# Modulation products moved from the rounds of the attentions to the merges of branches, half a group behind the gates of a half branch

## What is computed

```python
# first block, once
gates = jax.nn.sigmoid(proj("gates").reshape(b, s, N_BRANCH, D_MODEL) + b_gate[l])
projected = jnp.einsum('bsnc,ncd->bsnd', branches, w_branch[l])
mixed = jnp.sum(gates * projected, axis=2)
# second block, per layer i (DEPTH_2 = 2)
mod = jax.nn.silu(c) @ w_ada[i] + b_ada[i]
sh1, sc1, gt1, sh2, sc2, gt2 = jnp.split(mod[:, None, :], N_MOD, axis=-1)
modc = jax.nn.silu(c_ctx) @ w_ada[i] + b_ada[i]
ga, gb, gc = jnp.split(jax.nn.sigmoid(gates), N_BRANCH_2, axis=-1)
m = ga * (ya @ w_branch[0]) + gb * (yb @ w_branch[1]) + gc * (yc @ w_branch[2])
```

## Time and profile before

| | |
|---|---|
| median of 3 executions | 3238.53 us (3232.24 to 3244.42) |
| the profiled execution's own time | 3241.71 us |
| its span, first to last instruction | 3239.9 us |
| mean granted TensorE clock | 0.925 |
| busy: PE, PE weight loads, DVE, ACT, POOL | 82%, 55%, 36%, 27%, 1% of the span |
| DMA | 669.19 MB, mean 207 GB/s |
| modulation matmuls (L1499) | 192, in the trace as 384 records, 49.6 us busy |

### The profile page before, as it was taken

How to read it: one execution, slowest core, us unless ns; L and a number is a source line. 1 busy time by engine, 2 the same in 40 slices (tenths; PEclk the granted TensorE clock), 3 DMA queues, 4 the chain that set the end, 5 groups by cost and what they waited for, 6 DMA issues and landing times. The chain is left out here.

```text
span 3239.9 us, 36546 instructions
## 1 busy us (share of the span) xinstructions
PE 2658.2 (82%) x14364; PEld 1796.3 (55%) x14364; DVE 1169.5 (36%) x1596; ACT 882.3 (27%) x1314; POOL 39.9 (1%) x36
## 2 busy tenths in 40 slices
PE   6887898998998787889977778887887896787876
PEld 5666687998996464668753222223664894222222
DVE  4446544655753334344432001103444552000001
ACT  3344433544442232322221000002233432000001
POOL 0100000000000000000000000000000001000000
PEclk8888998999998898889978999998897997999999
DMA  4463532453542333112215999996211343999996
GB/s 154 157 257 113 198 130 92 178 185 123 188 159 91 150 136 130 50 69 100 85 46 224 404 405 407 403 414 260 78 52 50 142 165 147 413 410 409 411 410 269
DMA packets 92935, 669.19 MB, mean 207 GB/s; under 512 B 10320, under 2 KB 10496, under 8 KB 12800
## 3 DMA queue, kind: packets, MB, share of 16 engines
q1 hardware_dynamic: 90256, 654.67, 51.6%
q0 software_dynamic: 2272, 11.52, 1.0%
q10 hardware_dynamic: 272, 1.05, 0.1%
HBM read 666.13 MB, written 1.06 MB: 206 GB/s over the span
## 5 line engine op out<-in xcount | busy, mean ns | idle before, releaser
L1860 PE MATMUL ps<-ring,WK 128*64 128x512 f32 x3072 | 731.0, 605 | 171.2 <-DMA ring<-in_stream 147.1
L424 PE MATMUL ps<-A,piece_hi 128*128 128x256 f32 (+1 forms) x1952 | 618.5, 317 | 97.7 <-DVEq L358 33.1
L376 DVE TENSOR_TENSOR ring_lo<-ring,piece_hi 128x1024 fp32r<-128x1024 f32 x378 | 459.3, 1220 | 450.4 <-ACT piece_hi L369 449.3
L425 PE MATMUL ps<-A,piece_hi 128*128 128x256 f32 (+1 forms) x1952 | 612.5, 314 | 0.0
L426 PE MATMUL ps<-A,ring_lo 128*128 128x256 f32 (+1 forms) x1952 | 611.7, 313 | 0.0
L1860 PEld LDWEIGHTS ps<-ring,WK 128*64 128x64 f32 x3072 | 194.5, 137 | 674.2 <-DMA ring<-in_stream 371.9
L424 PEld LDWEIGHTS ps<-A,piece_hi 128*128 128x128 f32 x1952 | 384.7, 197 | 129.3 <-issue 59.2
L369 ACT ACTIVATE piece_hi<-ring 128x1024 fp32r<-128x1024 f32 x378 | 388.2, 1053 | 223.8 <-DVEq L450 131.9
L425 PEld LDWEIGHTS ps<-A,piece_hi 128*128 128x128 f32 x1952 | 385.6, 198 | 17.2
L426 PEld LDWEIGHTS ps<-A,ring_lo 128*128 128x128 f32 x1952 | 384.9, 197 | 18.1
L1980 DVE TENSOR_TENSOR WK<-WK,ps 128x512 f32<-128x512 f32 x32 | 22.0, 688 | 636.7 <-PE ps L1860 636.7
(11 more groups left out here) (252 smaller groups left out, 2447.6 us busy)
## 6 DMA issues: line engine op xcount, KB each, us to landing
ring<-in_stream SPq DMA_DIRECT2D x621, 1024.0 KB, 7.7
WK<-in_na_bias POOLq DMA_DIRECT2D x2, 2048.0 KB, 7.8
WK<-cum_scratch POOLq DMA_DIRECT2D x1, 2048.0 KB, 9.7
const<-in_const SPq DMA_DIRECT2D x1, 1267.0 KB, 11.7
WK<-in_x SPq DMA_DIRECT2D x1, 1024.0 KB, 5.4
WK<-in_mem SPq DMA_DIRECT2D x1, 1024.0 KB, 9.1
WK<-cum_scratch POOLq DMA_DIRECT2D x1, 1024.0 KB, 14.9
WK<-in_lru_w POOLq DMA_DIRECT2D x1, 1024.0 KB, 5.1
```

Of the source, the lines that this page charges most:

```text
L376: nc.vector.tensor_tensor(ring_lo[:, slot, at:at + PIECE], ring[:, slot, at:at + PIECE], f32(piece_hi[:, j, :]), ALU.subtract).then_inc(lo ...
L424: nc.tensor.matmul(out_, l[0], r[0], start=first, stop=False)
L425: nc.tensor.matmul(out_, l[0], r[1], start=False, stop=False)
L1860: last = nc.tensor.matmul(ps[64 * n:64 * n + 64, bank, :], lhs, piece[:, n * 512:n * 512 + 512], start=(k == 0), stop=(k == DC - 1))
```

## The change

The modulation products leave the attentions. They are done in the merges, in halves of a group: 8 raw pieces (k = 0 to 3 or 4 to 7) between the four gate banks and the four branch banks of a half branch. The first layer's groups go into half branches 1 to 6 of the first block's merge, the second layer's groups into half branches 0 to 5 of the merge in the second block's first layer. A group's turn (four matmuls, L1487) comes one half branch later, behind that half's raw pieces. The stream has its pieces in the new order. During these two merges the other banks go round a ring of six, since 6 and 7 belong to the modulation. The first block's merge is written out in place of its loop.

```diff
+ADA_HALF = 8
+ADA_MERGE = {0: (1, 2, 3, 4, 5, 6), 1: (0, 1, 2, 3, 4, 5)}
...
     for n in range(4):
         for h in range(2):
             fm(w_in, g0 + n * D + h * 512, g0 + n * D + h * 512 + 512)
+            ada(0, 2 * n + h)
             fm(x["w_branch"][0, n], h * 512, h * 512 + 512)
...
+        def merge_pe(pe, cur, branches, kc, n, ada=None):
             yh, yl = y_split(kc, n)
+            for i in range(branches):
                 for h in range(2):
+                    at = 2 * i + h
                     fm_banks(pe, cur, in_a()(n), n, 4)
+                    if ada is not None and ada_half(ada, at) is not None:
+                        ada_half_pe(pe, cur, ada, ada_half(ada, at))
+                    if ada is not None and ada_full_before(ada, at) is not None:
+                        ada_turn_pe(pe, 3 * ada + ada_full_before(ada, at) // 2)
                     if h == 0:
                         pe.wait_ge(y_lo, cur.base("y") + 1 + i)
                     fm_banks(pe, cur, lambda k: (yh[:, k, :], yl[:, k, :]), n, 4, kc)
-            merge_loop(pe, cur, branches, kc, one_branch)
+            if ada is not None and ada_full_before(ada, 2 * branches) is not None:
+                ada_turn_pe(pe, 3 * ada + 2)
...
 (merge_act)
                         read_bank(act, cur, True, op, piece=True)
+                    if ada is not None and ada_half(ada, 2 * i + h) is not None:
+                        past_raw(act, cur, ADA_HALF)
                     skip_fm(act, cur, 4, kc)
...
 (merge_dve)
                 for h in range(2):
+                    full = None if ada is None else ada_full_before(ada, 2 * i + h)
                     skip_fm(dve, cur, 4)
+                    if ada is not None and ada_half(ada, 2 * i + h) is not None:
+                        past_raw(dve, cur, ADA_HALF)
+                        if ada_half(ada, 2 * i + h) % 2 == 1:
+                            ada_rows_dve(dve, cur, ada, ada_half(ada, 2 * i + h))
...
+        def ada_half_pe(pe, cur, layer, half):
+            assert cur.p == ADA_PIECE[layer, half]
+            n, b = 3 * layer + half // 2, 6 + (3 * layer + half // 2) % 2
+            if half % 2 == 0:
                 pe.wait_ge(cs_ready, 1)
+                if n >= 2:
+                    pe.wait_ge(ada_added, n - 1)
+            for k in range(4 * (half % 2), 4 * (half % 2) + 4):
+                for q in range(4):
+                    if q % 2 == 0:
+                        piece = raw_piece(pe, cur)
+                        behind = cur.p - 1 - ADA_PIECE[layer, half]
+                        if behind < 4:
+                            pe.wait_ge(bank_free[cur.bank(cur.g - 4 + behind)], cur.bank_use(1, cur.g - 4 + behind))
+                    last = nc.tensor.matmul(ps[32 * q:32 * q + 32, b, :], CS[:, k, :], piece[:, q % 2 * 512:q % 2 * 512 + 512],
+                                            start=(k == 0), stop=(k == DC - 1))
+                    if (k, q) == (DC - 1, 3):
+                        last.then_inc(ada_full, 1)
+                    elif q % 2 == 1:
+                        raw_used(last, cur)
...
+        def ada_rows_dve(dve, cur, layer, half):
+            n = 3 * layer + half // 2
             dve.wait_ge(ada_full, n + 1)
+            dve.sem_inc(piece_used[(ADA_PIECE[layer, half] + ADA_HALF - 1) % 4], 1)
             if n > 0:
                 dve.wait_ge(ada_turned, n)
+            nc.vector.tensor_copy(ROWS[:, :], ps[:, 6 + n % 2, :]).then_inc(ada_taken, 1)
...
-            fox_pe(pe, cur, ada_with_pe(pe, cur, "fox"))
+            fox_pe(pe, cur)
...
-            merge_pe(pe, cur, 4, DC, T)
+            cur.set_ring(range(6))
+            merge_pe(pe, cur, 4, DC, T, ada=0)
+            cur.set_ring(range(NB))
```

More of the change, by code:

```diff
@@ L136, in __init__ @@
         self.g = 0
+        self.places = []
+        self.ring = list(range(NB))
+        self.turn = 0
+        self.uses = [0] * NB
         self.i = None
@@ L157, in split_use, with place, set_ring, used @@
         return v if self.i is None else v + self.i * (self.pieces_per // 4)
-    def bank(self):
-        return self.g % NB
-    def bank_use(self, k=0):
-        v = self.g // NB + k
+    def place(self, g):
+        while len(self.places) <= g:
+            b = self.ring[self.turn % len(self.ring)]
+            self.places.append((b, self.uses[b]))
+            self.uses[b] += 1
+            self.turn += 1
+        return self.places[g]
+    def set_ring(self, banks):
+        while len(self.places) < self.g:
+            self.place(len(self.places))
+        assert len(self.places) == self.g, (self.who, len(self.places), self.g)
+        self.ring, self.turn = list(banks), 0
+    def used(self, bank):
+        self.place(self.g - 1)
+        return sum(b == bank for b, _ in self.places[:self.g])
+    def bank(self, g=None):
+        return self.place(self.g if g is None else g)[0]
+    def bank_use(self, k=0, g=None):
+        v = self.place(self.g if g is None else g)[1] + k
         return v if self.i is None else v + self.i * self.banks_per
+    def taken_before(self):
+        return self.place(self.g)[1] > 0
 def one(i):
@@ L485, in tm_tile @@
         def tm_tile(pe, cur, t0, tt):
-            banks = [(cur.g + m) % NB for m in range(tt)]
+            banks = [cur.bank(cur.g + m) for m in range(tt)]
             for j in range(4):
@@ L1286, in lru_dve @@
             steps(nc.vector.tensor_tensor(LY, LXC[:, :, :], LG[:, :, :], ALU.mult))
-        def merge_loop(eng, cur, branches, kc, one_branch, steps=None, per=0):
-            if 2 * (4 + kc // 2) % (2 * R) == 0:
-                with loop(eng, cur, branches, pieces=2 * (4 + kc // 2), banks=16, steps=steps, steps_per=per) as i:
-                    one_branch(i)
-            else:
-                for i in range(branches):
-                    one_branch(i)
         def y_split(kc, n):
@@ L1351, in one_branch @@
                     dve.drain().then_inc(gate_used, 1)
-            merge_loop(dve, cur, branches, kc, one_branch, steps=steps, per=8)
+                    if full is not None:
+                        ada_add_dve(dve, 3 * ada + full // 2)
+            if ada is not None and ada_full_before(ada, 2 * branches) is not None:
+                ada_add_dve(dve, 3 * ada + 2)
             cur.add("merge", 2 * branches)
@@ L1508, in ada_rows_dve, with ada_turn_pe @@
+        def ada_turn_pe(pe, n):
+            pe.wait_ge(ada_taken, n + 1)
+            pick = ident.rearrange("p (q r) -> p q r", q=4)[:, :, 0:2]
+            for c in range(4):
+                last = nc.tensor.matmul(ps[:, 6 + n % 2, 8 * c:8 * c + 8], ROWS[:, c * P:(c + 1) * P], pick, start=True, stop=True)
+            last.then_inc(ada_turned, 1)
+        def ada_rows_dve(dve, cur, layer, half):
+            n = 3 * layer + half // 2
             dve.wait_ge(ada_full, n + 1)
-            dve.sem_inc(piece_used[(ADA_PIECE[layer, g] + ADA_GROUP - 1) % 4], 1)
+            dve.sem_inc(piece_used[(ADA_PIECE[layer, half] + ADA_HALF - 1) % 4], 1)
@@ L1561, in gmod_dve, with ada_full_before @@
+        def ada_full_before(layer, at):
+            half = ada_half(layer, at - 1)
+            return half if half is not None and half % 2 == 1 else None
         def gmod_dve(dve, steps, g, which):
@@ L2108, in _ @@
                 barrier(pe, cur)
-                att_pe(pe, cur, da_x, **({"after": ada_with_pe(pe, cur, "da_x")} if layer == 0 else {}))
+                att_pe(pe, cur, da_x)
                 barrier(pe, cur)
@@ L2193, in _ @@
                 barrier(act, cur)
-                att_act(act, cur, steps, na_x, **({"after": ada_with_act(act, cur, "na_x")} if layer == 0 else {}))
+                att_act(act, cur, steps, na_x)
                 barrier(act, cur)
                 if n > T:
-                    att_act(act, cur, steps, na_ctx, ada_with_act(act, cur, "na_ctx"))
+                    att_act(act, cur, steps, na_ctx)
                     barrier(act, cur)
@@ L2200, in _ @@
                 barrier(act, cur)
-                att_act(act, cur, steps, da_x, **({"after": ada_with_act(act, cur, "da_x")} if layer == 0 else {}))
+                att_act(act, cur, steps, da_x)
                 barrier(act, cur)
@@ L2287, in _ @@
                 dve.wait_ge(loads, 16 * LOADS["nab"][layer])
[L2288 removed]
+                att_dve(dve, cur, steps, na_x)
                 barrier(dve, cur)
                 if n > T:
[L2291 removed]
+                    att_dve(dve, cur, steps, na_ctx)
                     barrier(dve, cur)
@@ L2296, in _ @@
                 barrier(dve, cur)
-                att_dve(dve, cur, steps, da_x, **({"after": ada_with_dve(dve, cur, "da_x")} if layer == 0 else {}))
+                att_dve(dve, cur, steps, da_x)
                 barrier(dve, cur)
```

235 lines of the change are left out of this document (87 added, 148 removed).

## The result

| | before | changed |
|---|---|---|
| median of the runs that were compared | 3235.39 us (3227.95 to 3244.42, 4 runs) | 3311.02 us (3307.26 to 3322.69, 4 runs) |
| the profiled execution's own time | 3241.71 us | 3307.26 us |
| its span | 3239.9 us | 3305.1 us |
| mean granted TensorE clock | 0.925 | 0.919 |
| DMA | 669.19 MB | 669.34 MB |

The changed kernel is slower by 75.6 us, a ratio of 1.0239 with a 95% interval of 1.02 to 1.0278. The two profiled executions lie 65.2 us apart in span, since the one of before is slow for its kernel (3241.71 against a median of 3235.39) and the one of after fast for its own (3307.26 against 3311.02).

The account below looks back on a forecast made before the run. TensorE was taken as busiest everywhere, hardly resting in the merges, waiting on DVE and ACT in the attentions. Merges losing 147.8 us less 51.5 gained gave +96 on 3241.7: 3338, by the median 3335 us; range 3288 to 3370 (0.85).

Parts of the forecast that it names:

- The stall in the merges: Each of twelve half branches starts its branch 10.3 us after its gates, not 3.64; 123.6 us lost.
- R3: Last raw slot of a half branch, loaded only once the gates end; lands at T + 5.3, PE idle 2.5 us.
- B0: First branch slot, queued behind R3; lands at T + 7.8, is then split, and the branch starts at T + 10.3.
- 14 us or less from the last gate matmul to full rate: Sign expected in each of the twelve half branches of the merges.
- The clock: Rests before merge branches slow their matmuls: 2.4 us per narrow branch, 1.8 per wide; 25.2 us lost, lower bound 0.
- The rival by which the clock holds: Raw work between the two merge rests keeps the clock up, so 25.2 us fall away: 3310 us, chance 0.25.
- Turns and the unrolled loop: Merges: two group turns on the path cost 2.1 us; unrolling the first merge gives back 3.1 us.
- The attentions: All 192 modulation products leave fox, sb, na_x, na_ctx and da_x; 51.5 us gained after 4.4 for splits.
- I take 4.7: Time of a bare fox round, between 3.6 and 5.9 us; fox gains 21.1 us, bounds 12.7 and 28.8.
- na_ctx, 4.5 taken: Gain of attention na_ctx without products, at least 3.2 us by da_ctx, bounded at 7.
- The splits ahead of the stages: Three splits move ahead of each of four attention stages, costing 1.1 us each; 4.4 us lost.
- The loads hidden, and faster by fox: Two rivals: the ring hides merge loads, 3230 us (0.06); fox rounds at 3.6 us too, 3220 us (0.04).

Follow-up runs that it names:

- e2: Changed kernel with modulation products in full only at k = 0 of each group, 8 columns instead of 512 elsewhere; 3309.49 us, ratio 1.0239.
- e1: Changed kernel with raw pieces in 24 quarters of four, behind gates and behind branches, instead of twelve halves; 3256.42 us, ratio 1.0081 to the kernel before.
- e5: e1 with ACT splitting the branch's pieces while reading the last two gate banks; 3239.31 us, ratio 1.0039 to the kernel before.
- e3: Changed kernel with unread matmuls filling both rests of each half branch and a ring of five banks; 3295.85 us, ratio 1.0188 to the kernel before.
- e4: Changed kernel without the modulation: no products, turns or pieces of it, MOD zero; 3162.32 us, ratio 0.9786 to the kernel before.
- e6: e5 with only the first layer's modulation moved, the second layer's products back in its attentions; 3229.98 us, ratio 0.9978 to the kernel before.

## Why the prediction was right, and which terms were not

The forecast of 3335 us was 24 us above the measured 3311.02, which lies in the range; the side was right and so was the mechanism. About 3 of the 24 us are the kernel before, whose median was that much lower when the two were compared. By its own steps:

- **The stall in the merges** (12 x 10.3 = 123.6 us): right. 124.5 us in the trace. R3 landed at T + 5.0 (5.3 said), the idle before it was 2.3 us (2.5), B0 landed at T + 7.5 (7.8), the branch began at T + 10.0 (10.3). Three half branches took 11.3 to 11.5, because of a late load that the prediction did not have, and made up for the 0.3; that the sum fits to 1 us is in part luck. e2 shows that the 3.64 us of matmuls are no part of it, e1 and e5 that short stretches take the load's part of it away, and e5 that the split is a wait of its own. The sign "14 us or less from the last gate matmul to full rate" held in seven of the twelve; in the other five it was 14.1 to 17.2.
- **The clock** (25.2 us): 21.2 in the trace, and e3 gives 15 back in time. Each narrow branch lost 1.9 us on average and not 2.4, each wide one 1.6 and not 1.8. The step that sized it took one rest of 5 us; here the rest before the branch is 2.3 to 5.2 us, most often 3.9, and the loss a little smaller. It does not simply follow the rest: behind the 5.2 us of half branch 3 it was 2.5, behind the 5.1 us of the first wide branch 1.6, like that of the other wide ones. The rival by which the clock holds (3310 us) gave nearly the measured time, but it did not happen: no branch ran at 1.00. What it leaves out of the sum, 25 us, came instead from the attentions (about 20 more gained than said) and 4 us of clock. The Trainium skill ("TensorE: Matmul & The Clock Gate", "HAM oscillation") tells of a loop that ran at half rate for about 1.67 us behind each wait for a DMA, and counts half of that, about 0.83 us, as lost. The trace here differs: 3.1 to 5.7 us at the lower level behind each pair of rests, and 21.2 / 12 = 1.77 us lost. By the page's loss the clock term would be 12 x 0.83 = 10 us (an estimate from the page), half of what was measured.
- **Turns and the unrolled loop** (2.1 - 3.1 us): the two turns at the ends cost about 1.0, 0.8 in the first merge and 0.2 in the second, where the turn falls into the rest ahead of the output projection. The loop gave 4.6: the four runs of gates that held a wait of 0.55 to 1.05 us for a split took 12.6 to 13.0 us before and take 11.7 to 11.8 now. Merges in all: 143.3 measured, 147.8 said.
- **The attentions** (51.5 us gained): this is the term that failed. The trace has 66.4, with the restarts behind fox and sb 71.3, and e4 has some 65 in time.
  - fox, "I take 4.7": the bare rounds are 3.88 us. The step added half clock to the rounds, since PE rests much there; in fact all rounds but the first ran at full rate, and the stage came near the upper bound (27.7 of 28.8).
  - na_ctx, 4.5 taken, 7.5 measured, above the upper bound of 7, which was put together from the products and the splits. The value taken leaned on da_ctx, which runs at clock 0.56; na_ctx now runs at 0.86, so the comparison was one of two clocks.
  - da_x: 8.9 for 7.0, again against a twin at a lower clock (0.69, here 0.78). na_x, whose twin had the same clock (0.84), came out right, 11.4 for 11.5, but with luck: at the 57.6 us and clock 0.70 of e1 to e5 the gain would have been 7.0.
  - sb: 10.9 for 11.8.
  - The projections behind fox and sb were not in the sum. They gained 2.4 and 2.5 us. Behind fox PE no longer comes to them from a rest of 5 us, and all kernels without products in fox have the 2.4; the 2.5 behind sb came in some of them only.
  - The splits ahead of the stages (4.4 lost): 2.9. They lie ahead of the stages in the table, as longer rests of PE before the first scores: 1.58 to 2.71 us in sb, 0.94 to 2.08 in na_x, 1.78 to 2.44 in da_x, and 1.01 unchanged in fox.
- **The loads hidden, and faster by fox**: out. The rounds of fox came nearly at the rival's pace (3.88 us, 3.6 said), but a half cost 10.4 us in the merges, and the rival decided only under 3.9.

"The attentions give back under 35 us" and "the branches start 4 to 6 us behind the gates", which would have made it wrong, did not come.

## What to carry to other kernels

DMA share and PE's idle time in a stretch say how much work fits into it on average; whether a burst fits is set by the slots that stand loaded when it begins. Here eight pieces on a ring of four slots cost 12.1 us a time with the clock's share (124.5 + 21.2 over 12), for 3.64 us of matmuls, and two slots at a time cost 3.6 (e1), or 1.9 to 3.1 once the splits ran ahead (e5). When work is put ahead of something that needs preparation on other engines, let that preparation run before the work, or the next wait appears as soon as the first is gone (e1 to e5: 14 to 17 us). And a stage without the work is a good twin only at the same granted clock, which one trace does not fix (na_x: 53.2 or 57.6 us for the same code); take the rounds at full rate as one end.

## What was not expected of the hardware

- Loads of 1 MB that are issued within 2 us of each other mostly land 2.5 us apart, the first after 4.7 us, so the second takes 6.2 and the third 7.8; in three of twelve cases the second came 3.7 to 3.9 us behind the first. With the ring drained, the queue of loads and not the latency of one sets when work goes on.
- The clock fell between two rests of 2.3 and 3.9 us in spite of the matmuls between them; the eight records between them (1.06 us) were mostly still at full rate. Rests of 1.3 to 1.7 us behind every 12 to 15 us of work (e1) left both merges at 1.00 up to the last branch. In e3, with matmuls filled in, one branch of twelve began at the lower level behind a rest of 1.85 us; those behind 1.4 to 1.8 us did not.
- The same rounds of sb took 38.9 us at a granted clock of 0.91 (changed kernel), 40.3 at 0.83 (e6) and 41.0 at 0.79 (e5). The projection behind them took 46.3 us in the changed kernel, e1 and e6, and 49.0 in e2 to e5, about as before the change (48.8). The code there is the same in all of them. The times come in steps: sb is 38.9 in the changed kernel and e1, and 41.0 in all of e2 to e5; na_x is 53.2 in the changed kernel and 57.6 in all of e1 to e5. What decides between them was not tried.
- From one pair of raw matmuls to the next it was 0.43 to 0.45 us at 512 columns, and 0.03 to 0.08 at 8 columns (e2): the time of matmuls of this shape goes nearly all with their columns.
